# Second layer's attentions: two units turned in a row, two outputs in a row, each followed by one later unit's scores

## The reference

```
A: s = q k^T + bias(distance)      per head; masked sums over three dilated windows, one softmax
B: s = (qn kn^T + qr kr^T) * scale per head; causal, latent keys and values
p = exp(s - max) ; o = (p v) / sum(p)
mixed = [ o_A * silu(z_a), o_B * silu(z_b) ] ; x = x + mixed @ w_out
```

## Time and profile before

| | us |
|---|---|
| median of 3 runs | 2405.84 |
| lowest, highest | 2405.63, 2409.84 |
| span of the profiled execution | 2408.3 |

### The profile page before, as it was taken

The page is one execution under the profiler, slowest core; times in us unless marked ns, Lnnn a source line. Parts: engine busy times, 40 slices in busy tenths (PEclk is TensorE's granted clock), DMA queues, the critical chain, the costliest instruction groups (busy, mean ns, idle before and its releaser), DMA issues.

```text
span 2408.3 us, 36386 instructions
## 1 busy us (share of the span) xinstructions
PE 2351.4 (98%) x15466; PEld 1874.7 (78%) x15466; DVE 1185.9 (49%) x1460; ACT 785.0 (33%) x1217; POOL 1127.9 (47%) x771
## 2 busy tenths in 40 slices
PE   7999999999999989999999999999999999999999
PEld 6888888667778868878888887888778886666777
DVE  7811111564285354676766765333455216756621
ACT  4233331433322121254444441110433106564511
POOL 5477762333234268577777773434743221014221
PEclk9999999999999999999999999999999999999999
DMA  5233322101201056423222235222213112001024
GB/s 201 80 105 105 105 101 57 36 27 53 62 19 30 21 174 194 140 71 95 80 88 79 79 97 192 88 105 64 52 43 114 44 44 60 17 10 27 2 69 124
DMA packets 208251, 189.83 MB, mean 79 GB/s; under 512 B 16714, under 2 KB 186929, under 8 KB 207834
## 3 DMA queue, kind: packets, MB, share of 16 engines
q1 hardware_dynamic: 208090, 187.51, 24.7%
HBM read 141.31 MB, written 45.13 MB: 77 GB/s over the span
## 4 chain that ended last, share of the span: by engine, by line
PE 89%; DVE 5%; POOL 2%; ACT 2%; issue 1%; DMA 1%; SPq 0%; DVEq 0%; POOLq 0%; ACTq 0%
PE gp L1278 8%; PE gp L1280 8%; PE gp L1279 8%; PE sm L1840 3%; PE sm L1841 3%; PE sm L1839 3%; PE gp L1839 3%; PE gp L1840 3%; PE gp L1967 3%; PE gp L1841 3%; PE gp L1983 2%; PE gp L1424 2%; PE gp L1426 2%; PE gp L1425 2%; PE gp L1456 2%; PE sm L1456 2%
## 5 line engine op out<-in xcount | busy, mean ns | idle before, releaser
L982 POOL CAST w_hi<-w_raw 128x1024 fp32r<-128x1024 f32 (+1 forms) x97 | 107.3, 1106 | 690.4 <-PE gp L1280 317.5
L984 POOL TENSOR_TENSOR w_lo<-w_raw,w_hi 128x1024 fp32r<-128x1024 f32 (+1 forms) x105 | 284.5, 2709 | 8.3 <-ACT w_hi L2409 0.5
L1278 PE MATMUL gp<-h_hi,w_hi 128*128 128x512 f32 x656 | 260.7, 397 | 0.0
L1280 PE MATMUL gp<-h_hi,w_lo 128*128 128x512 f32 x656 | 255.6, 390 | 0.0
L1279 PE MATMUL gp<-h_lo,w_hi 128*128 128x512 f32 x656 | 255.4, 389 | 0.0
L1278 PEld LDWEIGHTS gp<-h_hi,w_hi 128*128 128x128 f32 x656 | 123.2, 188 | 29.8 <-issue 4.9
L1279 PEld LDWEIGHTS gp<-h_lo,w_hi 128*128 128x128 f32 x656 | 123.2, 188 | 27.4 <-issue 2.4
L1280 PEld LDWEIGHTS gp<-h_hi,w_lo 128*128 128x128 f32 x656 | 123.2, 188 | 25.8
L1192 POOL TENSOR_TENSOR w_lo<-w_sum,w_hi 128x512 fp32r<-128x512 f32 x66 | 95.8, 1452 | 43.6 <-ACT w_hi L2468 43.6
L2876 DVE TENSOR_TENSOR_SCAN sb_run<-sb_keep,ones_row 128x128 f32<-128x128 f32 (+7 forms) x32 | 74.1, 2355 | 84.8 <-POOL sb_keep L1030 84.8
L2633 ACT ACTIVATE att_s<-att_s,small 128x1024 f32<-128x1024 f32 (+7 forms) x128 | 98.8, 774 | 8.8 <-DVE small L3359 8.5
(11 more groups left out here) (661 smaller groups left out, 6423.8 us busy)
## 6 DMA issues: line engine op xcount, KB each, us to landing
w_raw<-in_w_in SPq DMA_DIRECT2D x67, 512.0 KB, 4.0
gate_in<-gates_spill SPq DMA_DIRECT2D x30, 512.0 KB, 4.2
gates_spill<-gate_out SPq DMA_DIRECT2D x28, 512.0 KB, 5.9
w_raw<-in_w_up SPq DMA_DIRECT2D x22, 512.0 KB, 5.0
up_raw<-in_w_up SPq DMA_DIRECT2D x22, 512.0 KB, 5.0
g_spill<-hid SPq DMA_DIRECT2D x22, 512.0 KB, 2.6
g_stage<-g_spill SPq DMA_DIRECT2D x22, 512.0 KB, 4.4
w_raw<-in_w_down SPq DMA_DIRECT2D x22, 512.0 KB, 3.8
```

The source lines that it names most:

```text
L982: pool.tensor_copy(w_hi[:, t % 2, 0:n], w_raw[:, t % 2, 0:n]).then_inc(s["w_high"], 1)
L984: pool.tensor_tensor(w_lo[:, t % 2, 0:n], w_raw[:, t % 2, 0:n], w_hi[:, t % 2, 0:n].bitcast(F32), ALU.subtract).then_inc(s["w_split"], 1)
L1278: pe.matmul(o, wh, hi[:, k0 + k, c], start=(k == 0), stop=False)
L1280: mm = pe.matmul(o, wl, hi[:, k0 + k, c], start=False, stop=(k == n - 1))
```

## The change

- The blocks come in the order (7, 0, 6, 1, 5, 2, 4, 3). Units 2g and 2g+1 are pair g; each pair has 18 blocks over both heads, in five chunks (4, 4, 4, 4, 2) that run on from the first unit into the second. Even r is copied by ACT, odd r by DVE.
- PE: Z of the first four units, in order; then for each pair g: T of both units, Z of the first unit of pair g+2, S of both and O of both, Z of the second unit of pair g+2.
- DVE: for each g its copies, scores of the first unit of g+2 (both heads), one reciprocal of four columns for pair g+1, the gate of pair g in two operations of 256 columns (two blocks of 128, a fixed distance apart), scores of the second unit of g+2. ACT: its copies of g, then all four exponentials of pair g+1.
- `att_pt` has 24 blocks, used from its beginning by every pair, instead of two halves of 16. Outputs take two places of 128 columns in the eighth bank, spread reciprocals the other two.
- `at_root`, `at_o`, `at_o_taken` count pairs.

```
             def turn(g):
                 if g == pairs[0]:
                     pe.wait_ge(s["at_s"], 2 * (at_pair(g)[0] + 2))
                 for r, _, pieces in at_chunks(g):
                     if r >= 3:
                         pe.wait_ge(*at_copies(r - 3))
                     for n, (u, k, hh) in enumerate(pieces):
                         if (k, hh) == (0, 0):
                             pe.wait_ge(s["at_p"], 2 * (u + 1))
                         mm = pe.transpose(...)
                     mm.then_inc(s["at_pt"], 1)
...
-                for n in (0, 2, 1, 3):
-                    z(units[n])
-                for u in units:
-                    turn(u)
-                    if u + 3 in units[4:]:
-                        z(u + 3)
-                    output(u)
+                for g in pairs[0:2]:
+                    for u in at_pair(g):
+                        z(u)
+                for g in pairs:
+                    a, b = at_pair(g + 2)
+                    turn(g)
+                    if g + 2 in pairs:
+                        z(a)
+                    output(g)
+                    if g + 2 in pairs:
+                        z(b)
...
+                exps(pairs[0])
+                for g in pairs:
+                    for r, i, pieces in at_chunks(g):
+                        if r % 2 == 0:
+                            (ACT's copy of chunk r)
+                    if g + 1 in pairs:
+                        exps(g + 1)
...
+                for g in pairs[0:2]:
+                    for u in at_pair(g):
+                        scores(u)
+                roots(pairs[0])
+                for g in pairs:
+                    for r, i, pieces in at_chunks(g):
+                        if r % 2:
+                            (DVE's copy of chunk r)
+                    a, b = at_pair(g + 2)
+                    if g + 2 in pairs:
+                        scores(a)
+                    if g + 1 in pairs:
+                        roots(g + 1)
+                    gated(g)
+                    if g + 2 in pairs:
+                        scores(b)
```

More of the change, by code:

```diff
@@ L631, in at_place, with at_pieces, at_chunks @@
             return u % 4 if u < UNITS else (0, 3, 2, 1)[u % 4]
[L633 to L641, removed]
+        def at_pieces(g):
+            return [(u, k, hh) for u in at_pair(g) for k in range(at_unit(u)[1] + 1) for hh in range(2)]
+        def at_chunks(g):
+            pieces = at_pieces(g)
+            return [(PAIR_CHUNKS * g + i // 4, i, pieces[i:i + 4]) for i in range(0, len(pieces), 4)]
         def at_copies(r):
[L645 to L650, removed]
+            return s[f"at_pt_copied{r % 2}"], r // 2 + 1
         def in_tile(n):
@@ L667, in head_bank, with at_o_bank, at_o_place, at_small @@
             return 4 if i == len(NORMED) - 1 else 2 * (i % 2)
[L669 to L678, removed]
+        def at_o_bank(kind):
+            return gp[:, 1, HALF + 2 * P * kind:HALF + 2 * P * kind + 2 * P].rearrange("p (n q) -> p n q", q=P)
+        def at_o_place(kind, u):
+            return at_o_bank(kind)[:, int(at_unit(u)[1] > 3), :]
+        def at_small(kind, u, hh):
+            c = 96 + 8 * kind + 2 * (u % 4) + hh
+            return small[:, c:c + 1]
+        def at_small_pair(kind, g):
+            c = 96 + 8 * kind + 4 * (g % 2)
+            return small[:, c:c + 4]
         @block.sync
@@ L1944, in _, with attention @@
             pe.wait_ge(s["n2_q"], 11)
-            def attention(units, scores, s_buf, pt_buf, v, evicted):
+            def attention(pairs, scores, s_buf, pt_buf, v, evicted):
                 def z(u):
@@ L1969, in turn, with output @@
                         mm.then_inc(s["at_pt"], 1)
[L1971 to L1979, removed]
+                def output(g):
+                    if g >= 1:
+                        pe.wait_ge(s["at_o_taken"], g)
+                    pe.wait_ge(s["at_root"], g + 1)
+                    for u in at_pair(g):
+                        for hh in range(2):
+                            pe.matmul(at_o_place(1, u)[C * hh:C * hh + C, :], at_small(2, u, hh).to_broadcast([P, C]),
+                                      ident[:, :], start=True, stop=True, skip_group_check=True)
+                    for r, i, pieces in at_chunks(g):
@@ L1980, in output @@
                         pe.wait_ge(*at_copies(r))
[L1981 to L1984, removed]
+                        for n, (u, k, hh) in enumerate(pieces):
+                            j, qb = at_unit(u)
+                            mm = pe.matmul(at_o_place(0, u)[C * hh:C * hh + C, :],
+                                           v[:, k, C * (2 * j + hh):C * (2 * j + hh) + C], pt_buf[:, i + n, :],
@@ L1998, in scores_a @@
+                for g in pairs:
[6 more added lines that the diff above has]
+                        z(b)
+                pe.wait_ge(s["at_s"], 2 * (at_pair(pairs[-1])[1] + 1))
+                pe.wait_ge(s["at_o_taken"], pairs[-1] + 1)
             def scores_a(u, j, qb):
@@ L2008, in scores_a @@
                             mm.then_inc(s["at_z"], 1)
-            attention(range(UNITS), scores_a, att_s, att_pt, v_2, P_LATENT)
+            attention(range(UNITS // 2), scores_a, att_s, att_pt, v_2, P_LATENT)
             pe.wait_ge(s["kv_split"], 1)
@@ L2091, in scores_b @@
                             mm.then_inc(s["at_z"], 1)
-            attention(range(UNITS, 2 * UNITS), scores_b, att_s, att_pt, v_b, P_OUT)
+            attention(range(UNITS // 2, UNITS), scores_b, att_s, att_pt, v_b, P_OUT)
             def turn_out(d):
@@ L2626, in _, with attention, exps @@
             logs_and_exps()
[L2628 to L2643, removed]
+            def attention(pairs, s_buf, pt_buf):
+                def exps(g):
+                    for u in at_pair(g):
+                        w = P * (at_unit(u)[1] + 1)
+                        for hh in range(2):
+                            act.wait_ge(s["at_s"], 2 * u + hh + 1)
+                            act.activation(s_buf[:, at_place(u), hh, 0:w], s_buf[:, at_place(u), hh, 0:w], ACT.Exp,
+                                           scale=-1.0, bias=at_small(0, u, hh), accum_out=at_small(1, u, hh)) \
+                                .then_inc(s["at_p"], 1)
+                exps(pairs[0])
+                for g in pairs:
+                    for r, i, pieces in at_chunks(g):
+                        if r % 2 == 0:
+                            n = len(pieces)
@@ L2644, in attention @@
                             act.wait_ge(s["at_pt"], r + 1)
-                            act.copy(pt_buf[:, u % 2, b[0]:b[0] + len(b), :],
-                                     bank(4 + r % 3)[:, 0:P * len(b)].rearrange("p (b q) -> p b q", q=P)) \
+                            act.copy(pt_buf[:, i:i + n, :], bank(4 + r % 3)[:, 0:P * n].rearrange("p (b q) -> p b q", q=P)) \
                                 .then_inc(s["at_pt_copied0"], 1)
-                        if u + 2 in units:
-                            exps(u + 2, n)
@@ L2651, in _ @@
-            attention(range(UNITS), att_s, att_pt)
-            act.wait_ge(s["at_o"], UNITS)
+                    if g + 1 in pairs:
+                        exps(g + 1)
+            attention(range(UNITS // 2), att_s, att_pt)
+            act.wait_ge(s["at_o"], UNITS // 2)
             for k in range(2):
@@ L2682, in _ @@
                     head_root(at[n - 1])
-            attention(range(UNITS, 2 * UNITS), att_s, att_pt)
+            attention(range(UNITS // 2, UNITS), att_s, att_pt)
             for d in range(KT - 1):
@@ L3350, in _, with attention, scores @@
                     add_rope(k_rope[:, :], 0, k_tmp[:, :])
-            def attention(units, table_of, s_buf, pt_buf, gate, step):
-                def scores(u, hh):
+            def attention(pairs, table_of, s_buf, pt_buf, gate, step):
+                def scores(u):
                     w = P * (at_unit(u)[1] + 1)
-                    dve.wait_ge(s["at_z"], 2 * at_turn(u) + hh + 1)
-                    tab = table_of(u, hh)
                     a = 0 if u < UNITS else HALF - w // 2
[L3359 to L3369, removed]
-                    for hh in range(2):
[L3371 to L3377, removed]
@@ new lines, in roots, with gated @@
+                def roots(g):
+                    dve.wait_ge(s["at_p"], 4 * (g + 1))
+                    dve.reciprocal(at_small_pair(2, g), at_small_pair(1, g)).then_inc(s["at_root"], 1)
+                def gated(g):
+                    dve.wait_ge(s["at_o"], g + 1)
+                    j = at_unit(2 * g)[0]
+                    low, high = sorted(at_unit(u)[1] for u in at_pair(g))
+                    z = gate[:, j, :].rearrange("p (n q) -> p n q", q=P)[:, low:high + 1:high - low, :]
+                    dve.tensor_tensor(z, z, at_o_bank(0)[:, :, ::step], ALU.mult).then_inc(s["at_half_gated"], 1)
+                    dve.wait_ge(s["at_half_gated"], g + 1)
```

(5 more changed lines are left out.)

48 lines of the change are left out of this document (27 added, 21 removed).

## The result

The changed kernel takes 2409.86 us (median of 20 runs, 2407.85 to 2423.83), the kernel before 2406.13 (median of 20: 19 runs from 2403.84 to 2409.84, and one at 4732.87, which does not move the median). The ratio is 1.0018, 95% interval 1.0011 to 1.0026, so +4.3 us with 2.6 to 6.3. Forecast were 2406.4 and "no change in measure"; the time is inside the range of 2398 to 2412, and the difference is just under the 4.8 us that I took for the limit of measure. With this many runs it is clear of zero, and it is more than the +0.6 of the sum.

The account below looks back on a forecast made before the run. PE was taken as the bound, with DVE near enough that its order matters. The terms -8.9 - 4.0 + 5.1 + 4.3 + 3.1 + 1.0 gave +0.6 us, so 2406.4 us from the median 2405.84, range 2398 to 2412.

Parts of the forecast that it names:

- Switches between kinds: PE's loop in both attentions: fewer steps between kinds of matmul save 0.28 us a pair over 32 pairs, -8.9 us.
- O to Z: PE's new step from making output to making scores: taken as 0.12 us, bounded by 0.11 and 0.20.
- Old waits gone: PE's waits for DVE to free score banks and for DVE's copies, in both attentions, go: -4.0 us.
- The ring: Transposes wait for DVE's late copies to free one of three PSUM banks: +5.1 us in A, +4.3 in B.
- Rival (a): The three PSUM banks do not hold PE up in the transposes: -9 us, 2397; chance 0.15.
- (b): Half the bank waits, DVE free 0.3 us earlier with gate operations of 0.29: -4.4 us, 2401.4; chance 0.17.
- The ends: Last pairs of both attentions: transposes wait 1.3 us for copies and the last gate is 0.26 longer, +3.1 us.
- The starts: First scores of each attention: +0.8 us in A, +0.2 in B; low clock in B -1.7 to +1.7 more.
- Rival (c): DVE's run of gate, second unit's scores and first copy becomes PE's pace: +8.3 us on the forecast, 2414.7; chance 0.13.
- Rival (d): The clock at the start of attention B falls twice: +1.7 to +3 us, 2409; chance 0.10.
- -10.9 for the switches: PE's loop: alternative saving, counting only tiling-mode changes, six a pair before and four after, at a mean of 0.17 us.

Follow-up runs that it names:

- experiment 1: Changed kernel with ACT copying chunks 0, 1 and 4 of every pair and DVE chunks 2 and 3: 2401.05 us, 0.9978 to the kernel before.
- experiment 5: Changed kernel with DVE copying chunks 1 and 3 of every pair and ACT 0, 2 and 4: 2406.25 us, 1.0002 to the kernel before.
- experiment 3: Changed kernel with the gate made unit by unit, four operations of 128 columns instead of two of 256: 2411.84 us, 1.0022 to the kernel before.
- experiment 2: Changed kernel with the reciprocal of each pair moved behind DVE's copies of that pair: 2409.69 us, 1.0013 to the kernel before.

## Why the prediction came out as it did

- **Switches between kinds, -8.9.** Right where it can be seen. O to Z cost 0.14, 0.02 more than taken and below the upper bound of 0.20. (The 0.054 for a record of O was rounded down: the slope is 1.53 / 28 = 0.0546, which leaves 0.10 for O to Z and for O to T alike, so the comparison stands.) T without waits is 2.19 (experiment 1), where I had 2.13. With the copies out of the way the loops and ends are 5.7 us (A) and 4.3 (B) shorter than before, 10.0 in all; the sum's first two terms, -12.9, with the 0.5 of the longer last gates and about 1 us of unit 0's S and O, which before lies ahead of the fifth Z, give -11.4. That is 1.4 us more than measured; the 0.06 of T in 32 pairs, 1.9 us, is more than the difference.
- **Old waits gone, -4.0.** Right in kind: no Z in the loop waits for scores. Not measured apart.
- **The ring, +9.4.** Right in kind, too high in size: the waits were worth 9.0 with the ends' share of 2.1, so 6.9 in the loops, which is where the 9.4 was counted. Of the 2.5 too much, 1.8 is T's own 2.19 in place of 2.13 in 30 pairs; most of the rest is pair (4,3) in A, worked out at 2.54 and measured at 2.45. The order of the pairs by wait, (6,1) worst, (7,0) least, and the difference between A and B came out, as did each T of experiment 5. Rival (a), in which the ring costs nothing, is out, and so is (b) by its mechanism: the gate took 0.42, though the waits fell short by nearly (b)'s 3 us.
- **The ends, +3.1.** 1.07 us of idle in T (1.3 was forecast), and 0.98 from the last gate to PE's next matmul in place of 0.71, so 0.27: 2.7 in all. Right to 0.4.
- **The starts, +1.0.** This is the term that failed. Their lengths at full clock were right to 0.2 us, but the clock was counted wrongly. "It may pay nothing or twice that: -1.7 to +1.7 more", I wrote. Yet T at 2175.2 is worked out from lengths at full clock (2.99 for a Z of 1024 columns), and the 2175.68 that it is set against holds before's 1.7 us of low clock. So "nothing" was already in the +0.2, and the band should have run from 0 to +3.4. On the mean of three profiles the changed kernel loses 2.8 us in B and 0.4 in A by low clock inside the starts, and 0.2 behind A's: 3.4, of which the sum had none. The kernel before loses 1.1 in B, 0.6 less than in the profile that I worked from. In A I had seen no low clock before and gave it none, though the same two gaps come there.
- **Rival (c)**, DVE's run as PE's pace, did not come, though its mechanism is real: experiment 3 makes the gate longer and pays 2.9 us. **Rival (d)**, low clock falling twice in B, came in two of three profiles, and I gave it 0.10. Its price, +1.7 to +3, holds the 2.8 of B's mean.
- **The balance.** The sum's +0.6, with 3.4 of low clock that it did not have and 0.6 for before's mean, would be +4.6. The profiles have +3.1, for the loops came out 1.5 better: 2.5 less in the ring and 0.4 less at the ends, against 1.4 less saved by switches and old waits. So the forecast is near the time in part by luck: two errors of opposite sign.

The rule that changing the tiling mode drains TensorE (the Trainium skill, "TensorEngine Tiling (Array Packing)", Tiling Modes) led to -10.9 for the switches, which is farther from what the loops show than -8.9. O to Z is such a change and showed 0.14 us, S to O isn't and showed 0.06 (S of 8 records with its step: 2029.42 - 2028.93 = 0.49, of which 0.43 is work). The rows agree with the rule; the price differs with what ran before (0.14 after O, 0.20 after Z), which a mean of 0.17 doesn't show.

## What to carry to other kernels

Joining two short stages in a loop saves switches, but can make the joined stage longer than the ring of buffers it writes through, as here with five chunks and three banks: count its chunks against the ring, and give the chunks whose buffer is wanted again within the same stage to the engine that has nothing queued ahead of them. Here that choice alone was worth 9 us, twice what the joining had lost. Look at the pipeline's start by itself: a large first item in a single buffer made gaps here, and a gap on TensorE can be paid twice, once as idle time and once as the low clock that followed it in many of these profiles.

## What the hardware showed that I had not expected

- Gaps of 1.4 to 2.2 us on PE were followed by 1.2 GHz in B's start in all three profiles of the changed kernel, and in A's in one of three, though A's gaps are the same to 0.02 us. The profiles of experiments 1, 2, 3 and 5 have the same gaps: B's start lost 1.7, 3.4, 1.7 and 5.1 us there, A's 0, 0, 3.4 and 1.3. In the kernel before, where no gap in B's start is longer than 0.8 us, 1.7 us were lost in two of three.
- 18 useless transposes in such a gap made the T behind it 2.25 us in place of 3.5 to 3.7.
- A vector operation of 256 columns in two runs of 128, read backwards from PSUM in A, costs the same 0.42 us as in B, where it is read forwards.
- The stretch ahead of A moved by 5 us from one profile of the kernel before to another (A's first Z at 1988.71, 1983.76, 1983.52): spans of single profiles can't settle a change of 0.2%.
